# Compressed blocks and gate logits as products with exchanged operands, and a new order of the value and block slots

## What is computed

```python
hn = rms_norm(x, g_mix)
proj = hn @ w_in                      # queries, keys, values, 12 gate logits, ...
# 31 blocks of 32 tokens, one every 16 tokens, from keys (k) and from values (v)
blocks = (t[:, idx] + pe).reshape(b, 31, 32 * 64)
kc = rms_norm(gelu(blocks_k @ w1_k) @ w2_k, g_k_cmp)    # w1: 2048 x 256, w2: 256 x 64
vc = gelu(blocks_v @ w1_v) @ w2_v
gates = sigmoid(gate_logits + b_gate)  # 3 branches x 4 heads for each token
q, k_slc, k_win, q_dil, k_dil = head-wise rms_norm(...)
o_a = gates[0] * attend(q, kc, vc) + gates[1] * attend(q, selected) + gates[2] * attend(q, window)
```

## Time and profile before

| what | value |
|---|---|
| median of three runs | 3338.1 us |
| the profiled execution's own time | 3334.2 us |
| its span | 3332.4 us, 1.8 us under its own time |
| TensorE busy | 3252.4 us, 98% |
| VectorE, ScalarE, GpSimd busy | 1558.9, 1201.6, 1480.3 us |
| mean granted TensorE clock | 0.987 |

### The profile page before, as it was taken

The page is one execution under the profiler, slowest core; times in us unless marked ns, Lnnn a source line. Parts: engine busy times, 40 slices in busy tenths (PEclk is TensorE's granted clock), DMA queues, the critical chain, the costliest instruction groups (busy, mean ns, idle before and its releaser), DMA issues.

```text
span 3332.4 us, 42986 instructions
## 1 busy us (share of the span) xinstructions
PE 3252.4 (98%) x15284; PEld 2646.5 (79%) x15284; DVE 1558.9 (47%) x2612; ACT 1201.6 (36%) x1871; POOL 1480.3 (44%) x724
## 2 busy tenths in 40 slices
PE   7999999999999999999999999999999999899998
PEld 5876778887777888788788878887888887788886
DVE  2244345512226556357655334557555454752223
ACT  3255433222335332356532243115332243552322
POOL 3460254445426444442544454445444454154442
PEclk9989999999999999999999999999999999999999
DMA  4310145542213555321455423102655322023331
GB/s 145 101 58 1 33 165 194 207 128 87 90 45 115 203 199 173 102 70 33 161 198 201 130 91 96 50 26 78 222 191 192 102 89 82 1 95 94 98 103 64
DMA packets 103107, 376.13 MB, mean 113 GB/s; under 512 B 11456, under 2 KB 11584, under 8 KB 102848
## 3 DMA queue, kind: packets, MB, share of 16 engines
q1 hardware_dynamic: 102816, 373.86, 34.0%
q0 software_dynamic: 160, 0.52, 0.1%
HBM read 372.24 MB, written 2.10 MB: 112 GB/s over the span
## 4 chain that ended last, share of the span: by engine, by line
PE 94%; DVE 3%; ACT 1%; issue 1%; DMA 0%; POOL 0%; SPq 0%; DVEq 0%; ACTq 0%; POOLq 0%
PE bank L739 21%; PE bank L741 21%; PE bank L740 21%; PE bank L832 3%; PE bank L827 2%; PE bank L828 2%; PE bank L978 2%; PE bank L783 2%; PE bank L784 2%; PE bank L785 2%; PE bank L1297 2%; PE bank L1002 1%; PE bank L927 1%; PE bank L876 1%; PE bank L1193 1%
## 5 line engine op out<-in xcount | busy, mean ns | idle before, releaser
L614 POOL TENSOR_TENSOR w_lo<-raw,w_hi 128x1024 fp32r<-128x1024 f32 x501 | 1224.8, 2450 | 1408.9 <-ACT w_hi L1377 1408.8
L1377 ACT ACTIVATE w_hi<-raw 128x1024 fp32r<-128x1024 f32 x501 | 526.8, 1057 | 1201.1 <-PE bank L741 1016.5
L739 PE MATMUL bank<-h_hi,w_hi 128*128 128x512 f32 x2264 | 883.8, 390 | 0.0
L740 PE MATMUL bank<-h_lo,w_hi 128*128 128x512 f32 x2264 | 881.5, 389 | 0.0
L741 PE MATMUL bank<-h_hi,w_lo 128*128 128x512 f32 x2264 | 881.3, 389 | 0.0
L739 PEld LDWEIGHTS bank<-h_hi,w_hi 128*128 128x128 f32 x2264 | 425.3, 188 | 90.6 <-issue 2.6
L740 PEld LDWEIGHTS bank<-h_lo,w_hi 128*128 128x128 f32 x2264 | 425.4, 188 | 89.0 <-issue 1.0
L741 PEld LDWEIGHTS bank<-h_hi,w_lo 128*128 128x128 f32 x2264 | 425.3, 188 | 88.8
L2489 DVE CUSTOM_DVE_ANT_0 ada_raw<-ada_raw,cond_row 128x1024 f32<-128x1024 f32 x192 | 308.9, 1612 | 279.8 <-DMA ada_raw<-ada 272.5
L739 PE MATMUL bank<-hid_hi,w_hi 128*128 128x512 f32 x880 | 344.0, 391 | 0.0
L741 PE MATMUL bank<-hid_hi,w_lo 128*128 128x512 f32 x880 | 342.4, 389 | 0.0
(11 more groups left out here) (371 smaller groups left out, 4092.7 us busy)
## 6 DMA issues: line engine op xcount, KB each, us to landing
raw<-weights SPq DMA_DIRECT2D x501, 512.0 KB, 3.5
ada_raw<-ada SPq DMA_DIRECT2D x192, 512.0 KB, 4.3
layer_const<-layer_const SPq DMA_DIRECT2D x5, 512.0 KB, 3.9
x<-x_t SPq DMA_DIRECT2D x1, 2048.0 KB, 7.9
cond_row<-cond SPq DMA_DIRECT2D x4, 512.0 KB, 4.3
y_t<-x SPq DMA_DIRECT2D x8, 256.0 KB, 2.0
tables<-big_const SPq DMA_DIRECT2D x1, 768.0 KB, 7.4
cols<-columns SPq DMA_DIRECT2D x1, 569.5 KB, 8.9
```

The source lines that it names most:

```text
L614: nc.gpsimd.tensor_tensor(w_lo[k % RING][:, :, :], raw[k % RING][:, :, :], w_hi[k % RING][:, :, :].bitcast(F32), ALU.subtract).then_inc(sm ...
L739: mm(out, w_hi[r][:, at, :], hi, start=first and at == 0, stop=False)
L740: mm(out, w_hi[r][:, at, :], lo, start=False, stop=False)
L1377: fn(w_hi[t % RING][:, :, :], raw[t % RING][:, :, :], ACT.Copy).then_inc(sm.hi_done, 1)
```

## The change

- Gate logits: VectorE splits `gate_w` into `gate_parts`, 44 columns with the high part in 0 to 11, the low part in 32 to 43 and zeros between. That is held, and `h_hi` and `h_lo` are streamed: 16 products of 512 columns. The result has gates in rows. It is copied to `gate_raw`, turned back by four transposes after the second tile of `linear`, and the bias is added after tile 6. The sigmoid moves behind sixteen splits.
- Block slots: the compressed blocks' input (high and low, 64 columns) is held and 256 weight columns are streamed, `w_hi` and `w_lo` for each of four chunks: 8 products a slot. The result `[64, 512]` is copied to `hid_raw` and turned back by four transposes (`hidden_turns`).
- The order of slots is `bbvbbbvbbbvv`. The wait ahead of the slots for the last eviction goes.
- All spreads stand before or between the products of slots 6 to 11, in banks 4 and 5, and the compressed chain's products stand around slots 10 and 11. Four of the five filling products go.
- VectorE evicts the four value tiles last, behind `mix_ready`. ScalarE clears `key_rows` at s = 6, and those rows now lie where the ada weights are loaded later, so SyncE waits for eight `att_out` before the first of those loads. GpSimd waits for the evictions before `dil_bias`.

```diff
-VALUES_AND_BLOCKS = "vbbvbbvbbvbb"
+VALUES_AND_BLOCKS = "bbvbbbvbbbvv"
-        key_rows = place("key_rows", [P, 2, 2, S], F32, h_at)
+        key_rows = place("key_rows", [P, 2, 2, S], F32, ada_at)
+                        sp.wait_ge(sm.att_out, 2 * TT)
+                pool.wait_ge(sm.lin_free, lin_total(("first",)) - 2 * FT - 2 * DT)
...
+            def gate_turns():
+                pe.wait_ge(sm.gate_kept_raw, 1)
+                for t in range(TT):
+                    op = turn(bank[7][:, 44 * t:44 * t + 44], gate_raw[:, t * P:(t + 1) * P], ident[0:44, 0:44])
+                op.then_inc(sm.gate_turned, 1)
...
-                pe.wait_ge(sm.lin_free, mt)
+                def hidden_turns():
+                    pe.wait_ge(sm.cmp_raw, 1)
+                    for a in range(4):
+                        op = turn(bank[6][:, 64 * a:64 * a + 64], hid_raw[:, a * P:(a + 1) * P], ident[0:64, 0:64])
+                    op.then_inc(sm.cmp_turned, 1)
+                def compressed():
+                    pe.wait_ge(sm.cmp_act, 1)
+                    ...
+                def key_norm():
+                    pe.wait_ge(sm.cmp_sq, 1)
+                    mm(norm, block64[0:HD, 0:HD], hid_pre[0:HD, 0, :], start=True, stop=True).then_inc(sm.cmp_mm, 1)
+                def spread(t):
+                    wait(pe, sm.g_out, n["gn"] + (t if t < 4 else t - 1))
+                    group_spread("in", items, t, bank[4 if t < 4 else 5 - t % 2])
+                def beside(s):
+                    if s == 10:
+                        return lambda t: spread(4) if t == 0 else spread(5) if t == 2 else None
+                    if s == 11:
+                        return lambda t: key_norm() if t == 0 else spread(7) if t == 1 else None
+                    return lambda t: None
...
-                        for c in range(8):
-                            both = blk_parts[:, kv, 8 * half_in + c, :, :]
-                            mm(out, w_hi[r][:, c, :], both.rearrange("p e n -> p (e n)"), start=first, stop=False)
-                            op = mm(out[:, 0:32], w_lo[r][:, c, :], both[:, 0, :], start=False, stop=last)
+                        for c in range(4):
+                            both = blk_parts[:, kv, 4 * q + c, :, :].rearrange("p e n -> p (e n)")
+                            for part_at, w in enumerate((w_hi, w_lo)):
+                                rows = w[r][:, 2 * c:2 * c + 2, :].rearrange("p a m -> p (a m)")
+                                op = mm(out, both, rows, start=q + c + part_at == 0, stop=q + c + part_at == 7)
...
-                        group_spread("in", items, s - 6, bank[4])
-                    elif s >= 10:
-                        late_spread(s - 6)
+                        spread(s - 6)
+                    if s == 9:
+                        hidden_turns()
+                    if s == 10:
+                        compressed()
+                        spread(6)
-                idle_products(7, 4)
...
-                    for t in range(TT):
-                        for c in range(DT):
-                            op = mm(bank[6][:, t * 12:(t + 1) * 12], h_tmp[:, c, t * P:(t + 1) * P], gw[:, c, :], ...)
+                    for c in range(DT):
+                        for at, h in enumerate((h_hi, h_lo)):
+                            op = mm(bank[6][0:44, :], gate_parts[:, c, :], h[:, c, :], start=c + at == 0,
+                                    stop=c + at == DT)
...
+                    if s == 9:
+                        act.wait_ge(sm.cmp_hidden, 1)
+                        fn(hid_cmp[:, :, :], hid_pre[:, :, :], ACT.Gelu_apprx_tanh).then_inc(sm.cmp_act, 1)
+                        act.wait_ge(sm.cmp_mm, 1)
+                        ...
+                        act.wait_ge(sm.cmp_mm, 2)
+                        ...
...
-                for t in range(4):
+                for t in range(len(items)):
                     if t == 3:
+                        dve.wait_ge(sm.slot_used, n["slot"] + VALUES_AND_BLOCKS.rindex("b") + 1)
+                        v.tensor_copy(hid_raw[:, :], bank[5][0:64, :]).then_inc(sm.cmp_raw, 1)
                         group_inverse("in", items, 1)
                     group_widen("in", items, t + 1)
-                    group_norm(items, t, (4,))
+                    group_norm(items, t, (4,) if t < 4 else (5, 4))
+                    if t == 3:
+                        dve.wait_ge(sm.cmp_turned, 1)
+                        v.tensor_reduce(hid_pre[:, :, :], bank[6][:, 0:256].rearrange("p (a e n) -> p a n e", a=4, e=2),
+                                        AX_X, ALU.add).then_inc(sm.cmp_hidden, 1)
...
                 op.then_inc(sm.mix_ready, 1)
+                for t in range(TT):
+                    v.tensor_copy(first_v[:, t, :], value_tile(t, len(VALUES_AND_BLOCKS))[:, :]).then_inc(sm.lin_free, 1)
```

More of the change, by code:

```diff
@@ L360, in program @@
         hid_pre = place("hid_pre", [P, 4, 32], F32, s1 + 5776)
+        hid_raw = place("hid_raw", [64, S], F32, s1)
+        gate_raw = place("gate_raw", [44, S], F32, s1 + 1024)
+        gate_parts = place("gate_parts", [P, DT, 44], F32R, s1 + 1536)
+        vcmp = place("vcmp", [32, 2, HD], F32, s1 + 5904)
         ml_w = small[:, 0:16]
@@ L755, in m_tile, with linear @@
                     c0 += m
-            def linear(tiles, hi, lo, chunks):
+            def gate_turns():
[3 more added lines that the diff above has]
+                op.then_inc(sm.gate_turned, 1)
+            def linear(tiles, hi, lo, chunks, after_second=None):
                 k, mt, per = n["slot"], n["mt"], len(chunks)
@@ L762, in linear @@
                         m_tile(k + q * per, mt + q, 0, 0, 0, hi, lo, chunks)
+                        if after_second and q == 1:
+                            after_second()
                     done = 4
@@ L785, in value_slot @@
                         op = mm(out, h_lo[:, d, tok], hi[:, c, :], start=False, stop=d == DT - 1)
-                    if s == TT - 1 and t < TT - 1:
-                        op.then_inc(sm.value_done, 1)
+                    if t < TT - 1:
+                        if s == TT - 1:
+                            op.then_inc(sm.value_done, 1)
+                        between(t)
                 op.then_inc(sm.slot_used, 1)
@@ L1056, in first_values @@
                 used = {"v": 0, "b": 0}
-                def late_spread(t):
-                    pe.wait_ge(sm.lin_free, mt + t - 3)
-                    group_spread("in", items, t, bank[(mt + t) % 4])
-                pe.wait_ge(sm.lin_free, mt)
+                w2 = [col("w2", 128 * kv, 128).rearrange("p (m d) -> p m d", m=2) for kv in range(2)]
+                key, value, norm = bank[6][0:HD, 256:288], bank[6][0:32, 288:352], bank[6][0:HD, 352:384]
+                def hidden_turns():
[5 more added lines that the diff above has]
+                    pe.wait_ge(sm.cmp_act, 1)
+                    for m in range(2):
+                        mm(key, w2[0][:, m, :], hid_cmp[:, m, :], start=m == 0, stop=m == 1)
+                    for m in range(2):
+                        op = mm(value, hid_cmp[:, 2 + m, :], w2[1][:, m, :], start=m == 0, stop=m == 1)
+                    op.then_inc(sm.cmp_mm, 1)
+                def key_norm():
[10 more added lines that the diff above has]
+                    return lambda t: None
                 for s, kind in enumerate(VALUES_AND_BLOCKS):
@@ L1073, in first_values @@
                         pe.wait_ge(sm.lo_done, k + s + 1)
-                        r, out = (k + s) % RING, bank[5][:, at // 2 * 64:at // 2 * 64 + 64]
-                        for c in range(8):
-                            both = blk_parts[:, kv, 8 * half_in + c, :, :]
-                            first, last = half_in == 0 and c == 0, half_in == 1 and c == 7
-                            mm(out, w_hi[r][:, c, :], both.rearrange("p e n -> p (e n)"), start=first, stop=False)
-                            op = mm(out[:, 0:32], w_lo[r][:, c, :], both[:, 0, :], start=False, stop=last)
+                        r, out = (k + s) % RING, bank[5][0:64, kv * 256:kv * 256 + 256]
+                        for c in range(4):
[3 more added lines that the diff above has]
+                                op = mm(out, both, rows, start=q + c + part_at == 0, stop=q + c + part_at == 7)
                         op.then_inc(sm.slot_used, 1)
                     if s == 0:
+                        pe.wait_ge(sm.gate_pre, 1)
                         for b, tile in ((0, 9), (1, 10)):
@@ L1326, in _ @@
                     mlstm_gates()
-                linear(len(tiles) - EARLY, h_hi, h_lo, [8])
+                linear(len(tiles) - EARLY, h_hi, h_lo, [8], gate_turns if part == "first" else None)
                 if part == "first":
@@ L2533, in _ @@
             dve.wait_ge(sm.const_loaded, 48)
+            gw = col("gate_w", 0, 96).rearrange("p (c g) -> p c g", c=DT)
+            link(v.memset(gate_parts[:, :, :].bitcast(F32), 0.0))
```

(3 more changed lines are left out.)

75 lines of the change are left out of this document (24 added, 51 removed).

## The result

Four runs of the changed kernel have a median of 3309.02 us (3306.16 to 3311.63), against 3339.99 for four runs of the kernel before. The ratio is 0.9907, with a 95% interval of 0.9895 to 0.9919: 0.93% faster, 31 us by the medians. The profiled execution took 3307.3 us, 26.9 less than that of before. The forecast was 3310 and 28 us less. A later set of four runs gave 3306.69 and a ratio of 0.9905.

The account below looks back on a forecast made before the run. TensorE, busy 3252.4 of 3332.4 us, and its lowered clock were taken as the bound. Gains of 8.0 (gates) and 21.2 (stage) less 1.0 behind it gave 28.2 us, so a median of 3310 us, range 3303 to 3322.

Parts of the forecast that it names:

- What bounds it: Whole kernel: TensorE, busy 3252.4 of 3332.4 us; only shorter TensorE work or less time at the lower clock gains.
- The gate step: Gate logits and linear work behind them: 13.7 us become 5.7 with 16 wide products, a gain of 8.0 us.
- Block products: Block slots: 64 products of 256 columns at 0.12 us each, 7.7 us (7.2 to 14.7) against 14.5 before.
- Waits: Stage of block and value slots: waits made by the new order, 4.2 us in all.
- the pause ahead of the scores: Tail: VectorE's last evictions end 2.6 us behind the last slot; a filling product hides 0.3, leaving 2.3.
- Item 7's squares: Slots after slot 6: clearing key_rows at s = 6 delays ScalarE's squares, so TensorE waits 0.9 us.
- the hidden turns: Behind slot 9: the turns wait for a 0.7 us eviction with a 0.4 us spread as cover, charged 0.5 us.
- The stage: From 146.16 to the first scores: 42.9 us of work and 4.2 of waits, 47.1 against 68.31, gain 21.2.
- The share by cause: Check on the stage's gain: 13.7 us of clock and 6.8 us of block products make 20.5 of it.
- Behind the stage: Start of the attention: GpSimd's convolution overlaps it and ScalarE has a split and table load; 1.0 us lost (0 to 3).
- one rival: Clock still falls between block slots and behind the end pause, narrow held operand included: 3313 to 3322 us, chance 0.22.
- The helpers: Rival: ScalarE, VectorE and GpSimd become the bound at block slots, costing 5 to 8 us, 3315 to 3318; chance 0.11.

Follow-up runs that it names:

- the first profile: Profiled execution of the changed kernel from its first four runs: 3307.3 us, 26.9 less than the profiled execution of the kernel before.
- one program's runs: Changed kernel with two value tiles evicted early and four filling products in the pause, clearing not moved: five runs of 3305.57 to 3318.96 us, ratio 0.9928.
- the run that spent some 30 us at half clock: Changed kernel with two value tiles evicted early, the clearing of key_rows moved to s = 9 and three filling products: 3316.69 us, ratio 0.9923.
- the changed kernel's second profile: Profile from running the changed kernel again, unaltered, beside two versions of the tail: runs of 3304.38, 3304.95, 3308.43 and 3309.23 us.

## Why the prediction was right

- **What bounds it** held. TensorE's busy time carried the gain, 26.4 of 26.9 us, in shorter work and in a clock that no longer falls.
- **The gate step**, 8.0 us: 7.9 in the profile, and 10 (6 to 14) by the run with the gates alone.
- **Block products**, 0.12 us each: 0.114 within a slot and 0.12 to 0.15 with the gaps at its ends. Eight slots took 8.8 us where I had 7.7.
- **Waits**, 4.2 us: the pause ahead of the scores was 2.57 us with its filling product, 2.6 by my sum, and for the reason given. Item 7's squares cost 0.6 (0.9), the hidden turns 0.2 (0.5). The spreads and the weights cost nothing.
- **The stage**: 47.1 forecast, 47.5 measured, where the products' 1.1 us more and the waits' smaller size (3.1 us instead of 4.2, the filling product left out) offset one another. That part of the closeness is luck. The share by cause holds as well: with wide products alone it is 53.2 us, so the products and the clock give 15.1 of its 20.8 us and the new order and chain 5.7.
- **Behind the stage** I charged 1.0 us, for GpSimd's work overlapping the attention and ScalarE's table load (1.28 us in the trace, at 184.80). In the first profile the attention was 2.5 us longer, with its clock at 0.95 by two falls, behind the pause and at 252. In the second, with no fall, it was 0.8 longer, and one of my two reasons shows in it: VectorE's small instruction stretched to 1.05 us beside GpSimd's, and TensorE waits for what follows. How much of the 0.8 this makes isn't shown; with six filling products the attention took 69.6 us, with the same GpSimd work beside it and waits of 1.1 us. The rest of the 2.5 is the clock, whose fall behind the pause I had among the rivals and not in the sum.
- **The rivals.** The clock did not fall in the stage, and behind the pause, where one rival had it fall, it fell in one of this kernel's two profiles. With 44 held columns the gate products ran at 1.00 (47.25 to 50.90), and with 64 the block slots did (the stage's 47.6 us), so a narrow held operand alone did not make the clock fall. The helpers didn't become the bound, even in a run of six block slots.

## What to carry to other kernels

Where one operand is narrow, hold it and stream the wide one: the block products cost what the narrow ones had cost each (0.114 us against 0.113), carried four to eight times the columns, and the clock stayed at 1.00 in them and in the dense work behind them. Turning the result back cost TensorE four transposes, about 0.4 us (168.93 to 169.31), and a wait of 0.2. Price a stretch of thin products by the granted clock of the stretch behind it too: behind the old gate logits it was 0.50 for 3.4 us. Before crediting or blaming an edit for a few microseconds, compare the granted clock of the runs and the length of the edited stage, for a part that nobody touched moved by more here: the attention took 69.6 us in one profile and 84.5 in another.

## What the runs showed of the hardware that was not expected

The clock fell from 1.00 to 0.50 in the middle of a long, steady stretch in which TensorE was 97 to 98% busy (72.62 of 74.60 us of the attention with narrow products in the new order, 71.38 of 72.60 in the changed kernel's). The same attention took 69.6 to 84.5 us in different profiles, and one program's runs differed by 13 us, with the mean clock between 0.987 and 0.993.

The traces show what went ahead of these falls. In eight profiles the clock fell in the middle or near the end of the attention, and each time TensorE's last wait before was one for VectorE's `att_tok_first`, of 0.35 to 0.98 us; the clock was at half before the wait ended or at most 1.3 us behind it. In the run that spent some 30 us at half clock it was this one, with the fall at about 215.3:

```profile
215.63 0.47 PE L1023 MATMUL bank<-kept,att_tok_first 128*128 128x128 f32 x1 [0.81 <-DVE att_tok_first L2113]
```

Such a wait isn't enough: the changed kernel's second profile has three, of 0.94, 0.81 and 0.47 us, and its clock stayed at 1.00. The 0.94 stands behind VectorE's instruction of 1.05 us beside GpSimd's, shown above, and the longest before a fall, 0.98 us in the run with both products in the old order, behind the same instruction at 1.09 us (215.93 to 217.02) beside GpSimd's (215.74 to 217.00). Why one such wait is followed by a fall and another is not stays open; no run changed the waits alone.
